# adaLN product turned round: silu(c) in four column groups, 512 columns of ada_w moving

## What is computed

```python
def modulate(x, g, shift, scale):
    return rms_norm(x, g) * (1.0 + scale) + shift

def adaln_params(cvec, w, b):
    m = jax.nn.silu(cvec) @ w + b
    return m.reshape(m.shape[:-1] + (N_MOD, D_MODEL))

def ffn_sublayer(x, shift, scale, gate, g_pre, g_post, wg, wu, wd):
    y = swiglu(modulate(x, g_pre, shift, scale), wg, wu, wd)
    return x + FFN_RES * gate * rms_norm(y, g_post)
...
    for layer in range(DEPTH):
        need_ctx = layer < DEPTH - 1
        mod = adaln_params(c, ada_w[layer], ada_b[layer])[:, :, None, :]
        modc = adaln_params(c_ctx, ada_w[layer], ada_b[layer])
...
        h = ffn_sublayer(h, mod[:, 0], mod[:, 1], mod[:, 2], g[0], g[1], ffn1_wg[layer], ffn1_wu[layer], ffn1_wd[layer])
...
        h = h + mod[:, 5] * rms_norm(y, g[3])
```

## Time and profile before

| | us |
|---|---|
| median of 3 runs (2696.25 to 2704.39) | 2701.06 |
| span of the profiled execution | 2664.7 |
| PE busy in it | 2428.4 |
| DVE busy | 921.7 |
| ACT busy | 768.6 |
| opening, to the first product of gate/up | 106.8 |

### The profile page before, as it was taken

One profiled execution on the slowest core, in us unless ns is written; L12 is line 12 of the kernel. 1 busy time (PEld: TensorE's weight loads), 2 busy tenths in 40 slices (PEclk: granted clock), 3 DMA queues, 4 the chain that ended last, 5 costly groups with the idle time before them and its releaser, 6 DMA issues.

```text
span 2664.7 us, 30086 instructions
## 1 busy us (share of the span) xinstructions
PE 2428.4 (91%) x12017; PEld 2031.8 (76%) x12017; DVE 921.7 (35%) x1268; ACT 768.6 (29%) x1098; POOL 177.7 (7%) x242
## 2 busy tenths in 40 slices
PE   8899999999999769699999997999998797677997
PEld 8688888887857657578888876888887675466997
DVE  0322222234122743452232232332223524545544
ACT  0412111224222323242222223222222524334443
POOL 2011111001000300010000001000000001000000
PEclk6699989998965555889999996999999798558999
DMA  7244443443300000234443332444333330003654
GB/s 240 61 128 133 146 130 107 119 130 106 94 16 1 1 1 0 64 109 128 118 124 114 90 111 75 134 126 128 101 87 110 87 82 1 0 1 95 173 161 123
DMA packets 363762, 250.25 MB, mean 94 GB/s; under 512 B 13384, under 2 KB 341412, under 8 KB 363680
## 3 DMA queue, kind: packets, MB, share of 16 engines
q1 hardware_dynamic: 343808, 181.89, 24.4%
q0 software_dynamic: 19872, 67.21, 8.1%
HBM read 248.02 MB, written 1.05 MB: 93 GB/s over the span
## 4 chain that ended last, share of the span: by engine, by line
PE 82%; DVE 7%; ACT 5%; DMA 3%; issue 2%; POOL 0%; SPq 0%; ACTq 0%; DVEq 0%; POOLq 0%
PE bank L273 19%; PE bank L275 19%; PE bank L274 19%; PE bank L1209 8%; PE bank L1226 2%; PE bank L1390 2%; PE bank L1367 2%; PE bank L1242 2%; PE bank L1420 2%; PE bank L1487 2%; PE bank L1443 1%; DMA ada_slot<-in_ada_w_dram 1%; PE bank L1379 1%; DVE rstd L737 1%; DVE w_lo L257 1%
## 5 line engine op out<-in xcount | busy, mean ns | idle before, releaser
L273 PE MATMUL bank<-u_hi,w_hi 128*128 128x512 f32 (+1 forms) x1872 | 706.2, 377 | 52.6 <-DVE u_lo L746 32.1
L274 PE MATMUL bank<-u_lo,w_hi 128*128 128x512 f32 (+1 forms) x1872 | 693.6, 371 | 0.0
L275 PE MATMUL bank<-u_hi,w_lo 128*128 128x512 f32 (+1 forms) x1872 | 693.3, 370 | 0.0
L257 DVE TENSOR_TENSOR w_lo<-raw,w_hi 128x2048 fp32r<-128x2048 f32 (+2 forms) x182 | 372.4, 2046 | 504.4 <-ACT w_hi L249 504.3
L273 PEld LDWEIGHTS bank<-u_hi,w_hi 128*128 128x128 f32 x1872 | 365.4, 195 | 119.3 <-issue 41.3
L275 PEld LDWEIGHTS bank<-u_hi,w_lo 128*128 128x128 f32 x1872 | 364.8, 195 | 60.2
L274 PEld LDWEIGHTS bank<-u_lo,w_hi 128*128 128x128 f32 x1872 | 365.8, 195 | 55.9
L249 ACT ACTIVATE w_hi<-raw 128x2048 fp32r<-128x2048 f32 (+2 forms) x182 | 311.4, 1711 | 168.1 <-PE bank L275 151.8
L1209 PEld LDWEIGHTS bank<-silu_c,ada_slot 128*128 128x128 f32 x1984 | 268.7, 215 | 27.4 <-issue 16.1
L1209 PE MATMUL bank<-silu_c,ada_slot 128*128 128x2 f32 x1984 | 260.9, 264 | 13.7 <-DMA ada_slot<-in_ada_w_dram 13.7
L273 PE MATMUL bank<-ht_hi,w_hi 128*128 128x512 f32 (+1 forms) x704 | 258.9, 368 | 5.1 <-DVE ht_lo L770 4.1
(11 more groups left out here) (221 smaller groups left out, 1968.8 us busy)
## 6 DMA issues: line engine op xcount, KB each, us to landing
ada_slot<-in_ada_w_dram POOLq DMA_DIRECT2D x124, 512.0 KB, 4.5
raw<-in_ffn_wg_dram SPq DMA_DIRECT2D x88, 512.0 KB, 4.0
raw<-in_ffn_wu_dram SPq DMA_DIRECT2D x88, 512.0 KB, 5.2
raw<-in_ffn_wd_dram SPq DMA_DIRECT2D x64, 384.0 KB, 3.7
raw<-in_ffn_wd_dram SPq DMA_DIRECT2D x64, 320.0 KB, 4.1
raw<-in_w_in_dram SPq DMA_DIRECT2D x40, 512.0 KB, 4.9
ada_first<-in_ada_w_dram SPq DMA_DIRECT2D x4, 2048.0 KB, 21.4
raw<-in_w_out_dram SPq DMA_DIRECT2D x16, 512.0 KB, 4.6
```

The source lines that it names most:

```text
L257: nc.vector.tensor_tensor(w_lo[s][:, 0:size], raw[s][:, 0:size], w_hi[s][:, 0:size].bitcast(F32), ALU.subtract).then_inc(lo_ready[s], 1)
L273: nc.tensor.matmul(acc, wh, xh, start=first, stop=False)
L274: nc.tensor.matmul(acc, wh, xl, start=False, stop=False)
L275: return nc.tensor.matmul(acc, wl, xh, start=False, stop=last)
```

## The change

The product is turned round. Now silu(c) stands and `ada_w` moves, 512 columns at a time. A **block** is 512 columns of `ada_w` (18 a layer, 36 in all; o is a block's place in `ADA_ORDER`), with all 1024 rows, 8 pieces k of 128. Piece k uses the 32 columns of `silu_c` that begin with its own two, and writes to partitions 32 (k % 4) and on of bank 6: four column groups of the array, of which each adds two pieces. Two rows of each group of 32 are wanted. ACT copies the bank to `ada_row`; `turn_block` then multiplies each 128 columns of it by `pick`, a matrix that has ones where those rows are, which adds the four groups and puts channels on partitions; DVE adds the bias and multiplies the gain (two small steps a block, from tables made once). There is one accumulator, so block o + 1 waits for the copy of block o (`ada_rows`).

A slot now holds a **quarter**: two pieces of 512 columns, again 512 KB, in pieces of 2 KB. The new places: 4 blocks in the opening (`first_block`), 11 beside gate/up of each FFN of layer 0 (half a block behind each unit), and 2 in each of the five boundaries (`TURN`). Nothing stands beside `down`, apart, or beside gate/up of layer 1. In the opening the norm sums come ahead of the blocks, and ACT copies the vectors and splits the first weights between the Sqrt and the rows. All loops of `steps` are written out.

```diff
@@ -23,8 +23,12 @@
-FIRST_GROUPS = 5
-FIRST_TILES = 4 * FIRST_GROUPS
+BLOCK = 4 * P
+QUARTERS = 4
+ADA_ORDER = ([(0, b) for b in (0, 2, 1, 3)] + [(0, b) for b in range(4, 2 * N_MOD)] + [(1, b) for b in range(2 * N_MOD)])
+FIRST_BLOCKS = 4
+BESIDE = {(0, 0): (4, 15), (0, 1): (19, 30)}
+TURN = {0: (15, 17), 1: (17, 19), 2: (30, 32), 3: (32, 34), 4: (34, 36)}
@@ -125,7 +140,9 @@
-        ada_slot = [own(f"ada_slot{s}", [P, KT, P]) for s in range(2)]
+        ada_slot = [own(f"ada_slot{s}", [P, KT // QUARTERS, BLOCK]) for s in range(2)]
+        ada_row = own("ada_row", [P, BLOCK])
+        pick = own("pick", [P, 2])
...
@@ -234,10 +251,8 @@
-            body(0)
-            with eng.Fori(1, count - 1) as i:
+            for i in range(count):
                 body(i)
-            body(count - 1)
...
+        def columns(o):
+
+            return bank[7] if FIRST_BLOCKS <= o and any(a <= o < b for a, b in BESIDE.values()) else bank[3]
+
+        def quarter(o, r):
+
+            n = QUARTERS * (o - FIRST_BLOCKS) + r
+            return n % 2, n // 2
...
-            for g in range(FIRST_GROUPS):
-                sp.dma_start(ada_first[g][:], ada_w[0].rearrange("(k p) f -> p k f", p=P)[:, :, g * 4 * P:(g + 1) * 4 * P])\
-                    .then_inc(first_loaded[g], 16)
+            for o in range(FIRST_BLOCKS):
+                b = ADA_ORDER[o][1]
+                sp.dma_start(ada_first[o][:], ada_w[0].rearrange("(k p) f -> p k f", p=P)[:, :, b * BLOCK:(b + 1) * BLOCK])\
+                    .then_inc(first_loaded[o], 16)
...
@@ -376,20 +387,19 @@
+            def ada(o, r):
+                layer, b = ADA_ORDER[o]
+                slot, k = quarter(o, r)
+                wait(pool, ada_used[slot], k)
+                pool.dma_start(ada_slot[slot][:], src[:, 2 * r:2 * r + 2, b * BLOCK:(b + 1) * BLOCK]).then_inc(ada_loaded[slot], 16)
...
+            ada_run(BESIDE[0, 0])
+            ada_run(TURN[0])
+            mixer_constants(0)
+            gla(0)
+            pool.wait_ge(mixer["y_tok_ready"], 2 * (TOK // LAT))
+            ada(TURN[1][0], 0)
+            ada(TURN[1][0], 1)
+            pool.wait_ge(post["ss_done"], 2)
+            for name in MIX:
+                nc.gpsimd.sem_clear(mixer[name])
+            ada(TURN[1][0], 2)
+            ada(TURN[1][0], 3)
+            ada_run((TURN[1][0] + 1, TURN[1][1]))
+            ada_run(BESIDE[0, 1])
+            ada_run(TURN[2])
+            ada_run(TURN[3])
+            mixer_constants(1)
+            gla(1)
+            pool.wait_ge(mixer["y_tok_ready"], 2)
+            ada_run(TURN[4])
@@ -491,8 +501,20 @@
+            def ada_row_out(o):
+
+                if o < FIRST_BLOCKS:
+                    act.wait_ge(ada_summed, o + 1)
+                else:
+                    slot, n = quarter(o, QUARTERS - 1)
+                    act.wait_ge(ada_used[slot], n + 1)
+                wait(act, ada_turned, o)
+                nc.scalar.activation(ada_row[:], ada_acc[:], ACT.Copy).then_inc(ada_rows, 1)
+
             def norm_in(layer, q, z, T):
 
+                if z - 1 in TURN:
+                    ada_row_out(TURN[z - 1][0])
...
                 mean_root(T, norm["sq_used"], norm["rms_ready"], KT * z + KT)
+                if z == 0:
+                    vectors()
+                    for o in range(FIRST_BLOCKS):
+                        ada_row_out(o)
+                if z - 1 in TURN:
+                    ada_row_out(TURN[z - 1][0] + 1)
...
                 def body(i):
+                    if (layer, q) in BESIDE and i >= 1:
+                        ada_row_out(BESIDE[layer, q][0] + i - 1)
                     for j in range(2):
...
@@ -739,7 +782,15 @@
+                if z - 1 in TURN:
+                    modulation(TURN[z - 1][0])
                 invert(norm["rms_ready"], z + 1, norm["rstd_ready"], z + 1, T)
+                if z == 0:
+                    mod_tables()
+                    split_lo(dve, 0)
+                    for o in range(FIRST_BLOCKS):
+                        modulation(o)
+                dve.wait_ge(mod_done, MODS_BEFORE[z])
...
                 low(KT - 1)
+                if z - 1 in TURN:
+                    modulation(TURN[z - 1][0] + 1)
...
+                        if (layer, q) in BESIDE and i >= 1 and j == 0:
+                            modulation(BESIDE[layer, q][0] + i - 1)
...
@@ -810,36 +866,32 @@
...
+            def modulation(o):
+
+                layer, b = ADA_ORDER[o]
+                at = b // 2 * KT + b % 2 * 4
+                bias, gain = (vec1[layer][:, w, at:at + 4].unsqueeze(2).to_broadcast([P, 4, 2]) for w in range(2))
+                this = mod[layer][:, b // 2, b % 2 * 4:b % 2 * 4 + 4, :]
+                dve.wait_ge(ada_turned, o + 1)
+                nc.vector.tensor_tensor(this, columns(o)[:, 0:8].rearrange("p (k s) -> p k s", s=2), bias, ALU.add)\
+                    .then_inc(mod_part, 1)
+                dve.wait_ge(mod_part, o + 1)
+                nc.vector.tensor_tensor(this, this, gain, ALU.mult).then_inc(mod_done, 1)
...
@@ -1201,51 +1242,58 @@
-            def ada_tile(j, order, k):
-
-                s = order % 2
-                pe.wait_ge(ada_loaded[s], 16 * k + 16)
-                for kk in range(KT):
-                    last = nc.tensor.matmul(mod_acc[:, bass.ds(j * 2, 2)], ada_slot[s][:, kk, :], silu_c[:, kk:2 * KT:KT],
-                                            start=(kk == 0), stop=(kk == KT - 1))
-                last.then_inc(ada_used[s], 1)
...
+            def ada_quarter(o, r):
+
+                slot, n = quarter(o, r)
+                pe.wait_ge(ada_loaded[slot], 16 * n + 16)
+                if r == 0:
+                    pe.wait_ge(ada_rows, o)
+                for kk in range(2):
+                    k = 2 * r + kk
+                    lane = 32 * (k % 4)
+                    last = nc.tensor.matmul(ada_acc[lane:lane + 32, :], silu_c[:, 2 * k:2 * k + 32], ada_slot[slot][:, kk, :],
+                                            start=(k < 4), stop=(k >= 4))
+                last.then_inc(ada_used[slot], 1)
...
+            def first_block(o):
+
+                pe.wait_ge(first_loaded[o], 16)
+                wait(pe, ada_rows, o)
+                for k in range(KT):
+                    lane = 32 * (k % 4)
+                    last = nc.tensor.matmul(ada_acc[lane:lane + 32, :], silu_c[:, 2 * k:2 * k + 32], ada_first[o][:, k, :],
+                                            start=(k < 4), stop=(k >= 4))
+                last.then_inc(ada_summed, 1)
+
+            def turn_block(o):
+
+                pe.wait_ge(ada_rows, o + 1)
+                wait(pe, mod_part, o)
+                for t in range(4):
+                    last = nc.tensor.matmul(columns(o)[:, 2 * t:2 * t + 2], ada_row[:, t * P:(t + 1) * P], pick[:, 0:2],
+                                            start=True, stop=True)
+                last.then_inc(ada_turned, 1)
 
             def norm_in(z, T):
...
+                    if z - 1 in TURN:
+                        o = TURN[z - 1][0]
+                        if k == 3:
+                            turn_block(o)
+                        if k == 1 or k == 5:
+                            ada_quarters(o + 1, (k // 4,))
+                if z - 1 in TURN:
+                    o = TURN[z - 1][0] + 1
+                    ada_quarters(o, (2, 3))
+                    turn_block(o)
...
+                        if f == 1:
+                            pe.wait_ge(mod_part, COLUMNS_FREE[z])
...
-                        if ("beside", layer, q) in ada_parts:
-                            _, j0, count, order = ada_parts["beside", layer, q]
-                            per = count // FT
-                            for t in range(per):
-                                o = order + j * per + t
-                                ada_tile(i * (2 * per) + (j0 + j * per + t), o, o // 2 + i * per)
+                        if (layer, q) in BESIDE:
+                            o = BESIDE[layer, q][0] + i
+                            if j == 0 and i >= 1:
+                                turn_block(o - 1)
+                            ada_quarters(o, (2 * j, 2 * j + 1))
...
             def sum_squares(z, T):
+                if z in TURN:
+                    ada_quarters(TURN[z][0], (0, 1))
                 pe.wait_ge(post["ysq_added"], KT * z + KT)
                 nc.tensor.matmul(bank[7][:, 0:T], ones[:], sq_sum[:, 0:T], start=True, stop=True).then_inc(post["ss_done"], 1)
-                turn_tiles(z, 0, 2)
+                if z in TURN:
+                    ada_quarters(TURN[z][0], (2, 3))
...
-                        if (layer, q) == (0, 0):
-                            _, j0, _, order = ada_parts["down"]
-                            ada_tile(i * 2 + (j0 + t), order + t, order // 2 + i)
+                        if i + t == 0 and (layer, q) in BESIDE:
+                            turn_block(BESIDE[layer, q][1] - 1)
...
@@ -1516,19 +1569,23 @@
-            for j in range(FIRST_TILES - 4):
```

(31 more changed lines are left out.)

161 lines of the change are left out of this document (40 added, 121 removed).

## The result

| | before | after |
|---|---|---|
| median, us | 2698.65 (4 runs, 2686.68 to 2704.39) | 2498.64 (4 runs, 2487.89 to 2501.52) |
| span of the profiled execution | 2664.7 | 2496.6 |
| run less span, profiled execution | | 2498.38 - 2496.6 = 1.8 |

The ratio is 0.9295, 95% interval 0.924 to 0.9351: 200 us less, where 2511 us was forecast (190 us less than 2701.06) with a range of 2465 to 2600. But one term, the 36.4 us said to lie outside the program, was put in the wrong place altogether: span to span the two traces differ by 168 us only.

What follows compares the result with a forecast made beforehand. TensorE was taken as the bound, with 82% of the chain. Stage gains and losses summed to 189.6 us, taking the 2664.7 us span to 2475; with 36.4 us outside it, 2511 us, range 2465 to 2600.

Steps and rivals of the forecast that it cites:

- 36.4 us: Profiled span's distance below the median of 2701.06 us, taken as constant time outside the program and added to the forecast span.
- Half block: Beside gate/up, four matmuls in four column groups run together: 1.35 us with shape changes, bounds 0.9 and 4.2.
- Opening: Up to the first product: norm sums hide under loads, blocks follow the weights at 1.2 GHz; 64 us, gain 42.8.
- FFN stages: FFN 1 and 2 of layer 0 at 405.5 us each, FFN 1 of layer 1 at 367.2; gains 74.5, -1.3 and 37.4.
- Boundaries: Between stages, two blocks cost 3 us over a bare boundary: 32.8 us for the first four, about 21 for the last.
- Boundary z = 1: Boundary behind layer 0's mixing, costed like the others at 32.8 us, a gain of 4.0 us.
- z = 4: Layer 1's narrow boundary, 17.43 us before: two rounds of DMA don't fit, a loss of 4.0 us.
- A: Rival for half blocks: column groups overlap in pairs only, 2.1 us each, 2563 us in all; chance 0.10.
- B: Rival for half blocks: column groups run one after another, 3.9 us each, 2669 us in all; chance 0.08.
- C: Rival for the whole program: written-out loops starve PE, 41 us more, 2552 us in all; chance 0.05.
- D: Rival for half blocks: one after another with the clock falling, 7.1 us each, slower at 2821 us; chance 0.04.
- E: Rival for the opening: late weights hold the ada rows, costing 12 us, 2523 us in all; chance 0.03.

Runs made afterwards that it cites:

- after_again: The changed kernel, unchanged, run again beside the kernel with all three follow-up moves; five runs, median 2496.04 us.
- before_again: The kernel before, unchanged, run again for a second trace; two runs, 2704.46 and 2711.13 us, traced span 2702.8 us.
- before_written_out: The kernel before with every turn of every loop written out, nothing else; twelve runs, median 2692.66 us, ratio 0.9857.
- one_group: The changed kernel with all eight pieces of a block in one column group of 32 instead of four; two runs, median 2631.02 us.
- before_norm_first: The kernel before with the opening reordered (norm sums first, then 20 two-column tiles) and the old adaLN product; ten runs, median 2694.84 us, ratio 1.0032.
- gate_last: The changed kernel with the last two blocks moved from the boundary ahead of the last FFN to beside its first gate/up units; 2438.44 and 2498.85 us.

## Why the prediction came out, step by step

- **Half block, 1.35 us (0.9 to 4.2).** It was 1.23: 0.99 for itself, so starts 0.08 and not 0.15, and changes of shape 0.24 and not 0.3. The row groups pointed the right way. A unit took 12.1 and 12.9 us, not 12.3 and 13.2. The bare unit was 10.88 us and not 10.95, since a tile alone in a unit costs 1.85 us and not 1.78. The drain that the Trainium skill (TensorEngine Tiling (Array Packing), Key Properties) names costs at most 0.24 us here for two changes.
- **Opening, 64 us.** 61.3, by the mechanism told: the weights at 38.8 ahead of the first row, then block after block. Said was half clock in all of it; two of the three blocks behind the wait had it. after_again's was 65.7.
- **FFN stages, 405, 405 and 367.** 401.0, 399.4 and 367.6. The third is right to 0.4 us: 21 tiles at 1.78 are what went. The first two are the sizes of the half block and the turn (0.79 and not 0.9). The clock is 0.99 in all three, so behind two tiles in a unit the fall was real and went with them.
- **Boundaries, 33 us four times and 21.** 30.4, 30.6 and 29.5 were below it: two blocks cost under 1 us over the bare 29.80 (0.5 to 1.7 us over the 28.95 that it took in before_again). There was more clock in them (0.80, 0.80 and 0.89; before 0.74, 0.61 and 0.71). In the third the norm sums' records took 593 ns at the median and not 697; in the others the medians don't differ so, and that the clock is the cause isn't shown. Boundary z = 1, 38.3, is the step that failed: the change was costed there as elsewhere, and POOL's clears, which the diff shows between quarters 1 and 2, were not counted: 4.0 us were to be gained, and 1.5 were lost. z = 4, 25.5 for 21.4: two rounds of DMA don't fit, as said, 8 us and not 4.
- **The projection behind z = 0** lost 3 us (121.06 against 118.00), and wasn't in the sum: PE waits for u_lo 4.8 us in all there, and 0.6 in the first trace of before. In the last 8 us of the boundary the clock was 0.88 and not 0.51; that this is why it gets ahead of DVE is argued, not shown.
- **36.4 us outside the program.** Wrong: 1.7 us are. That the forecast came out all the same is luck in this term: added to the span as a constant it stands for the 38 us that the attention of layer 1 takes longer at half clock, and the ordinary executions of both kernels have those. The sign of it stood in the first trace: its PEclk row reads 9855 in the mixer of layer 1 (slices 33 to 36) and 65555 in that of layer 0 (12 to 16), which is the same code.
- **The sum.** By stage against the first trace its nine terms are 45.5 + 79.0 + 4.8 + 37.0 + 4.7 - 1.5 + 39.1 + 0.3 - 8.1 = 200.8 us, said 189.6. Eight of the nine terms are off by 2 to 6 us, six one way and two the other, so that the sum came within 11 us is in part their cancelling.
- **The rivals.** A and B are excluded by the 0.99 us of four groups beside the 1.84 and 3.55 of two and one; C by before_written_out; D by the clock of 1.00 with one group; E's condition wasn't met, as the weights landed at 38.8 us; the wait that it speaks of was in the forecast, and taking it away brought 13.6 us.

## What to carry to other kernels

A product of few vectors with a large matrix belongs on the array with the vectors standing and the matrix moving, spread over the column groups. The groups bring the price down (a block 3.0 us with four, 7.7 with one, against 7.4 for its four tiles at full clock), and the wide moving side kept the clock in gate/up (0.99 with four groups, 1.00 with one, 0.94 with two tiles a unit). Before a span is compared with a median, compare the span with its own run; where they differ by more than a few us, the trace is of another kind of execution, and its clock row shows the stage. In a boundary count everything on every queue between two issues, semaphore clears too, and ask of each engine's in-order wait what stands behind it that could go ahead.

## What was not expected of the hardware

- Four fp32 matmuls of 512 columns in four column groups start 6 or 7 ns apart and take 0.99 us; two lots in two groups take 1.84, four in one group 3.55.
- The clock fell from 1.00 to 0.50 in a stretch where PE was busy all of the time, with matmuls of two columns (18 to 60 us of before_norm_first). It was 1.00 over the whole of FFN 1 of layer 0 with matmuls of 32 x 512 columns one after another between the products (one_group).
- The same program's attention stands at either level in different executions: the mixer of layer 1 took 210 or 248 us (before), that of layer 0 294 or 347 (gate_last, after). The kernel before ran from 2661.7 to 2715.4 us in 19 runs. What decides it is open; nothing was tried on it.
